# Moving TensorE's waits for the next projection ahead of the last chunk of the one before

## Chip, cores and metric

The kernel runs on one core of one Trainium2 chip. The metric is device time in microseconds (us) of one execution, from its first to its last instruction and what the measurement puts around them; the median of several runs counts.

## What is computed

Two transformer-like blocks, one layer each, on one sequence of 512 tokens with 1024 features, all in float32. Cut to the parts that matter here:

```python
# first block
h = modulate(rms_norm(x, g_ffn1), sh1, sc1)             # sh, sc, gt come from silu(c) @ w_ada + b_ada
x = x + 0.5 * gt1 * swiglu(h, w1_gu, w1_down)           # 1024 -> 2 x 2816 -> 1024
h = modulate(rms_norm(x, g_mix), sh2, sc2)
...                                                     # short convolution, windowed attention
merged = sigmoid(z_conv) * y_conv + sigmoid(z_attn) * y_attn
x = x + gt2 * (merged @ w_out)
h = modulate(rms_norm(x, g_ffn2), sh3, sc3)
x = x + 0.5 * gt3 * swiglu(h, w2_gu, w2_down)
# second block
x = x + token_mixer(rmsnorm(x, norm_mix), ...)          # HGRN and mLSTM heads
x = x + cross_attention(rmsnorm(x, norm_xattn), rmsnorm(mem, norm_mem), w_xq, w_xkv, w_xo)
h = rmsnorm(x, norm_mlp)
x = x + jnp.square(jax.nn.relu(h @ w_up)) @ w_down      # 1024 -> 4096 -> 1024
```

## The kernel before

Features lie on the 128 partitions, tokens along the row, so x is eight chunks of 128x512. Every projection is cut into units. A **unit** gives 128 output features for all 512 tokens in one PSUM bank: for each of its chunks of 128 input features (eight, or six in the down projections of the third part of a feed-forward) three matmuls accumulate, high weights by high input (L1439), high weights by low input (L1440), low weights by high input (L1441). That is how float32 accuracy comes from matmuls on a shorter format. There are 353 units, numbered v in the order in which they run: first feed-forward 0 to 67, then mix, convolution, its projection, attention's projection (`V_AP`, 120 to 135), output projection (`V_WO`, 136 to 143), second feed-forward (144 to 211), the mixer's (212 to 256), cross-attention's (257 to 280), its output projection (`V_XO`, 281 to 288) and the MLP (`V_MLP`, 289 to 352).

A unit's weights pass through four engines, each with its instructions in a fixed order, tied by semaphores:

- SyncE loads unit v's weights into one of four `raw` buffers (L342) when the buffer's last user is through.
- ScalarE (`split`, L428) rounds them into `whi[v % 2]` once unit v-2 has been multiplied (`unit_done`).
- VectorE (`split`, L820) writes the remainder into `wlo[v % 2]` and counts up `w_split`.
- TensorE (`unit`) waits for `w_split` and for `evac[v % 2]`, which says that bank v % 2 has been emptied of unit v-2, then multiplies, and counts up `unit_done` with the last matmul.

The two waits (L1428 to L1430) stand at the head of `unit`, ahead of the first chunk. Only the first unit that reads a new operand waits chunk by chunk as well (`first`), since its input is still being made.

What empties the bank depends on the stage. In a feed-forward, pairs of units (gate, up) are emptied by ScalarE (silu, L489) and VectorE (multiply, L917), and the product is split into `ghi` (L502) and `glo` (L923). A down projection's unit is added to x by VectorE (`residual`: L829 with a scale, L867 without). In the MLP an up unit goes through ScalarE (relu, L793), VectorE (square, L1405), ScalarE (`ghi`, L795) and VectorE (`glo`, L1407).

A feed-forward runs in three parts of 8, 8 and 6 chunks of 128 hidden features: 16, 16 or 12 gate and up units in a hardware loop, then eight down units. During the first feed-forward VectorE also multiplies the modulation weights `w_ada` (`ada`, one instruction L882 and seven L829 on 128x128, from the same four raw buffers), and TensorE adds each up with a matmul of one column (L1450) between two units. In a down projection VectorE's order for unit v is: split of v+1, residual of v, and for the first four units one `ada`. SyncE issues the loads in a fixed order too, so that the load of a down unit stands behind the load that waits for an `ada`.

The change touches `unit`, at the head of TensorE's program, and `mlp` at its end; both run through TensorE's loops (`Fori`), where the awaited counts are worked out in registers.

Of the kernel before, what the change touches and what calls it, by code (L numbers as in the profile page):

```python
# [24 lines left out]
DC = D // P  # L25
# [21 lines left out]
V_FFN_LEN = 2 * (FF // P) + len(FF_PARTS) * DC  # L47
# [3 lines left out]
V_AP = V_CP + 16  # L51
V_WO = V_AP + 16
V_FFN = (0, V_WO + DC)
V_GATE = V_FFN[1] + V_FFN_LEN
# [6 lines left out]
V_XO = V_XQ + DC  # L61
V_MLP = V_XO + DC
# [7 lines left out]
def raw_of(v):  # L70

    if v >= V_FFN_LEN:
        return v + N_ADA
    part = v // 24
    base, k, gu = ADA_HEAD_N + PART_LEN * part, v - 24 * part, 2 * FF_PARTS[part]
    return base + 2 * k if k < gu + ADA_TAIL else base + gu + ADA_TAIL + k


def raw_of_ada(a):
    if a < ADA_HEAD_N:  # L80
        return a
    part = sum(a >= start for start in ADA_PART[1:])
    return ADA_HEAD_N + PART_LEN * part + 2 * (a - ADA_PART[part]) + 1


def chunks_of(v):
    return FF_PARTS[2] if any(base + 60 <= v < base + V_FFN_LEN for base in V_FFN) else DC
# [27 lines left out]
def build(nc, x_in, mem_in, vec_in, con_in, rope_in, mask_in, w8_in, w6_in, out):  # L115
    with ExitStack() as ctx:
# [3 lines left out]
        def sem(name):  # L120
            return ctx.enter_context(nc.semaphore(name))
# [118 lines left out]
        w_split = sem("w_split")  # L240
        unit_done = sem("unit_done")
        evac = [sem(f"evac{i}") for i in range(2)]
# [92 lines left out]
        @block.sync  # L335
        def _(sp):
            sp.dma_start(vec[:], vec_in).then_inc(small_in, 16)

            def load(u, w, kc=DC):

                src = w8_in if kc == DC else w6_in
                sp.dma_start(raw[u % 4][:, 0:kc * P], src[w]).then_inc(landed[u % 4], 16)  # L342

            user = {raw_of(v): (w_split, v + 1) for v in range(V_END)}
            user |= {raw_of_ada(a): (ada_step, DC * (a + 1)) for a in range(N_ADA)}

            def load_at(u, w, kc=DC):
                if u >= 4:  # L350
                    sp.wait_ge(*user[u - 4])
                load(u, w, kc)

            for u in range(4):
                load_at(u, u)
            with sp.Fori(1, ADA_HEAD_N // 4) as i:
                for k in range(4):
                    sp.wait_ge(ada_step, DC * (k - 3) + 4 * DC * i)
                    load(k, 4 * i + k)
            for part, kc in enumerate(FF_PARTS):  # L360
                v0, a0 = 24 * part, ADA_PART[part]
                u0 = raw_of(v0)
                for u in range(u0, u0 + 8):
                    load_at(u, u)
                with sp.Fori(1, kc // 2) as i:
                    for k in range(4):
                        sp.wait_ge(w_split, v0 + k - 1 + 4 * i)
                        load(u0 + 2 * k, u0 + 2 * k + 8 * i)
                        sp.wait_ge(ada_step, DC * (a0 + k - 1) + 4 * DC * i)
                        load(u0 + 2 * k + 1, u0 + 2 * k + 1 + 8 * i)  # L370
                for c in range(DC):
                    u = raw_of(v0 + 2 * kc + c)
                    load_at(u, u if kc == DC else c, kc)
                    if c < ADA_TAIL:
                        load_at(u + 1, u + 1 if kc == DC else u0 + 4 * kc + c)

            def run(v0, v1, w0, kc=DC):

                for k in range(4):
                    load_at(raw_of(v0 + k), w0 + k, kc)  # L380
                if v1 - v0 >= 8:
                    with sp.Fori(1, (v1 - v0) // 4) as i:
                        for k in range(4):
                            sp.wait_ge(w_split, v0 + k - 3 + 4 * i)
                            load(raw_of(v0 + k), w0 + k + 4 * i, kc)
                for k in range((v1 - v0) // 4 * 4, v1 - v0):
                    load_at(raw_of(v0 + k), w0 + k, kc)

            down2 = V_FFN[1] + 60
            row0 = raw_of(V_MIX) - DC  # L390
            run(V_MIX, down2, row0)
            run(down2, V_GATE, DC, FF_PARTS[2])
            run(V_GATE, V_END, row0 + down2 - V_MIX)
            sp.wait_ge(stored, 16 * DC)
# [1025 lines left out]

        @block.tensor
        def _(pe):
            def unit(v, src, dv=0, n=S, first=None, rows=None):


                kc = chunks_of(v)
                hi, lo = src
                pe.wait_ge(w_split, v + 1 + 4 * dv)  # L1428
                if v >= 2 or not isinstance(dv, int):
                    pe.wait_ge(evac[v % 2], v // 2 + 2 * dv)  # L1430
                wh, wl = whi[v % 2], wlo[v % 2]
                outs = ((bank[v % 2], 0),) if rows is None else rows
                for dst, off in outs:
                    m = P if rows is None else 8
                    for c in range(kc):
                        if first is not None:
                            pe.wait_ge(first[0], first[1] + c + 1)
                        ws = slice(c * P + off, c * P + off + m)
                        nc.tensor.matmul(dst[0:m, 0:n], wh[:, ws], hi[:, c, :], start=c == 0, stop=False)  # L1439
                        nc.tensor.matmul(dst[0:m, 0:n], wh[:, ws], lo[:, c, :], start=False, stop=False)  # L1440
                        ins = nc.tensor.matmul(dst[0:m, 0:n], wl[:, ws], hi[:, c, :], start=False, stop=c == kc - 1)  # L1441
                ins.then_inc(unit_done, 1)
# [17 lines left out]
            def swiglu(f):  # L1460
                base, j0 = V_FFN[f], J_FFN[f]
                n = (N_FFN1, N_FFN2)[f]
                for part, kc in enumerate(FF_PARTS):
                    v0, j1, a0 = base + 24 * part, j0 + 8 * part, ADA_PART[part]

                    def body(i, first=None):
                        for k in range(4):
                            unit(v0 + k, H, i, first=first if k == 0 else None)
                            if f == 0 and (k >= 2 or not isinstance(i, int)):
                                ada(a0 + k - 2, 4 * i)  # L1470

                    if f == 0:
                        pe.wait_ge(mods_done, (2, 6, 7)[part])
                    body(0, (h_ready, H_AT[n]) if part == 0 else None)
                    with pe.Fori(1, kc // 2) as i:
                        body(i)
                    if f == 0:
                        for a in range(a0 + 2 * kc - 2, a0 + 2 * kc):
                            ada(a)
                    for c in range(DC):  # L1480
                        unit(v0 + 2 * kc + c, G, first=(op_ready, j1) if c == 0 else None)
                        if f == 0 and 2 <= c < 2 + ADA_TAIL:
                            ada(ADA_PART[part + 1] - ADA_TAIL + c - 2)
# [25 lines left out]
            for j in range(12):  # L1509
                unit(V_MIX + j, H, first=(h_ready, H_AT[N_MIX]) if j == 0 else None)  # L1510
                if 1 <= j <= 10:
                    rotate(j - 1)
                if j == 11:
                    v = V_MIX + 10
                    pe.wait_ge(evac[v % 2], v // 2 + 1)
                    turn_values(gate_in[0], bank[4], NB)
# [38 lines left out]
            v = V_MIX + 11  # L1555
# [176 lines left out]
            for c in range(DC + 4):  # L1732
                if c < DC:
                    unit(V_XQ + c, H, first=(h_ready, H_AT[N_XATTN]) if c == 0 else None)
                if c >= 2 and c % 2 == 0 and c < DC + 2:
                    hh = c // 2 - 1
                    v = V_XQ + c - 1
# [23 lines left out]


            def mlp(i, first):
                for c in range(DC):
                    unit(V_MLP + c, H, 4 * i, first=first if c == 0 else None)
                for c in range(DC):
                    unit(V_MLP + DC + c, G, 4 * i, first=(op_ready, J_MLP + DC * i) if c == 0 else None)

            mlp(0, (h_ready, H_AT[N_MLP]))
            with pe.Fori(1, MLP_PARTS) as i:  # L1770
                mlp(i, None)
# [126 lines left out]
```

## Time and profile before

| | |
|---|---|
| time, median of 3 runs | 2567.57 us |
| the runs | 2567.57, 2564.54, 2578.78 us |
| profiled execution, first to last instruction (span) | 2575.9 us |
| profiled execution's own time | 2578.78 us, the only one of the three above the span |
| TensorE busy | 2282.6 us, 89% |
| VectorE busy | 1320.8 us, 51% |
| ScalarE busy | 813.1 us, 32% |
| mean granted TensorE clock | 0.950 |
| HBM read | 226.45 MB |

PE is TensorE's matmuls, PEld its weight loads (LDWEIGHTS), DVE VectorE, ACT ScalarE, POOL GpSimd, SPq the queue that issues loads. Matmuls overlap: each is drawn as lasting 0.39 us or so, while the next starts 0.23 us after it, so the pace is read from starts and not from durations. A releaser behind "<-" is the instruction whose semaphore ended a wait.

### The profile page before, as it was taken

To read this page: it belongs to the slowest core of one execution; us is meant where nothing else is said; L and a number is where in the kernel's file an instruction comes from. 1 tells how busy PE (TensorE), PEld (TensorE's weight loads), DVE (VectorE), ACT (ScalarE), POOL (GpSimd) and SP (SyncE) were. 2 spreads that over 40 slices of the span, in tenths; PEclk is the share of its full clock that TensorE was granted. 3 is DMA by queue.
4 is the path that set the end of the run, shared out by engine and by line. 5 is a ranking of instruction groups with operands and counts; after the bars stand their busy time and mean duration, and the time that the engine had idled before them with its cause. 6 is when DMAs were issued, how large, how long until landed. Compare 5 with 4: busy or idle time off the path is not lost.

```text
span 2575.9 us, 27144 instructions
## 1 busy us (share of the span) xinstructions
PE 2282.6 (89%) x9880; PEld 1783.2 (69%) x9880; DVE 1320.8 (51%) x2228; ACT 813.1 (32%) x1174; POOL 83.3 (3%) x63
## 2 busy tenths in 40 slices
PE   1799999899999998999996788878868789899998
PEld 1588888676667776888883666655527666688886
DVE  7776768545554434333334455556554344534443
ACT  1322222323343323222234322224433343422332
POOL 1000000000000001000002000000000101000001
PEclk9899999999999999999998899988878999999999
DMA  6354544222122232333321111101103311233322
GB/s 230 122 173 162 177 164 165 91 79 66 58 72 80 78 90 74 98 98 98 95 88 56 58 41 40 39 28 41 46 3 98 115 50 63 74 94 104 93 95 73
DMA packets 63316, 229.92 MB, mean 89 GB/s; under 512 B 7024, under 2 KB 7152, under 8 KB 62960
## 3 DMA queue, kind: packets, MB, share of 16 engines
q1 hardware_dynamic: 61344, 220.90, 27.2%
q0 software_dynamic: 720, 5.57, 0.5%
q10 hardware_dynamic: 1152, 2.10, 0.2%
q8 instruction: 65, 1.06, 0.2%
q14 instruction: 35, 0.29, 0.0%
HBM read 226.45 MB, written 2.10 MB: 89 GB/s over the span
## 4 chain that ended last, share of the span: by engine, by line
PE 79%; DVE 12%; ACT 4%; issue 2%; POOL 1%; DMA 1%; DVEq 0%; SPq 0%; ACTq 0%; POOLq 0%
PE bank L1439 23%; PE bank L1440 23%; PE bank L1441 23%; DVE work L829 3%; PE bank L1643 2%; DVE normed L829 1%; PE bank L1526 1%; DVE hlo L829 1%; PE bank L1682 1%; PE bank L1551 1%; DVE work L1355 1%; PE bank L1666 1%; DVE wlo L820 1%; POOL square_sum L413 1%; PE bank L1709 1%
## 5 line engine op out<-in xcount | busy, mean ns | idle before, releaser
L1439 PE MATMUL bank<-hhi,whi 128*128 128x512 f32 (+1 forms) x1936 | 779.1, 402 | 80.5 <-DVE wlo L820 38.2
L1440 PE MATMUL bank<-hlo,whi 128*128 128x512 f32 (+1 forms) x1936 | 752.7, 389 | 0.0
L1441 PE MATMUL bank<-hhi,wlo 128*128 128x512 f32 (+1 forms) x1936 | 751.4, 388 | 0.0
L820 DVE TENSOR_TENSOR wlo<-raw,whi 128x1024 fp32r<-128x1024 f32 (+1 forms) x353 | 428.5, 1214 | 329.0 <-ACT whi L428 326.4
L1439 PEld LDWEIGHTS bank<-hhi,whi 128*128 128x128 f32 x1936 | 369.9, 191 | 197.9 <-issue 69.7
L428 ACT ACTIVATE whi<-raw 128x1024 fp32r<-128x1024 f32 (+1 forms) x353 | 368.0, 1042 | 434.9 <-PE bank L1441 392.2
L1441 PEld LDWEIGHTS bank<-hhi,wlo 128*128 128x128 f32 x1936 | 370.0, 191 | 76.2 <-issue 0.9
L1440 PEld LDWEIGHTS bank<-hlo,whi 128*128 128x128 f32 x1936 | 370.9, 192 | 73.2 <-issue 6.1
L1439 PE MATMUL bank<-ghi,whi 128*128 128x512 f32 x864 | 340.1, 394 | 6.2 <-DVE wlo L820 5.8
L1440 PE MATMUL bank<-glo,whi 128*128 128x512 f32 x864 | 336.6, 390 | 0.0
L1441 PE MATMUL bank<-ghi,wlo 128*128 128x512 f32 x864 | 336.5, 389 | 0.0
L829 DVE SCALAR_TENSOR_TENSOR work<-raw,cact,work 128x128 f32<-128x128 f32 x504 | 183.2, 363 | 17.9
L1439 PEld LDWEIGHTS bank<-ghi,whi 128*128 128x128 f32 x864 | 162.5, 188 | 42.1 <-DVE wlo L820 7.6
L1440 PEld LDWEIGHTS bank<-glo,whi 128*128 128x128 f32 x864 | 162.6, 188 | 33.7 <-issue 0.8
L1441 PEld LDWEIGHTS bank<-ghi,wlo 128*128 128x128 f32 x864 | 162.3, 188 | 34.0
L413 POOL TENSOR_TENSOR square_sum<-square_sum,square 128x512 f32<-128x512 f32 (+1 forms) x54 | 80.2, 1485 | 1932.7 <-ACT square L444 1929.5
L1643 PE MATMUL bank<-work 128*128 128x128 f32 (+1 forms) x512 | 78.5, 303 | 33.7 <-DVE work L1225 30.8
L829 DVE SCALAR_TENSOR_TENSOR xT<-bank,mods,xT 128x512 f32<-128x512 f32 x56 | 42.0, 750 | 123.8 <-PE bank L1441 123.8
L867 DVE TENSOR_TENSOR xT<-bank,xT 128x512 f32<-128x512 f32 x48 | 33.2, 691 | 137.9 <-PE bank L1441 137.9
L1643 PEld LDWEIGHTS bank<-work 128*128 128x128 f32 x512 | 68.2, 200 | 42.1 <-DVE work L1242 23.4
L502 ACT ACTIVATE ghi<-opnd 128x512 fp32r<-128x512 f32 (+1 forms) x44 | 27.8, 632 | 214.6 <-DVE opnd L917 214.6
L489 ACT ACTIVATE gate_in<-bank 128x512 f32<-128x512 f32 x44 | 26.4, 599 | 145.1 <-PE bank L1441 145.1
(186 smaller groups left out, 1595.2 us busy)
## 6 DMA issues: line engine op xcount, KB each, us to landing
raw<-w SPq DMA_DIRECT2D x409, 512.0 KB, 3.6
raw<-w SPq DMA_DIRECT2D x16, 384.0 KB, 3.1
xT<-x_t POOLq DMA_DIRECT2D x1, 2048.0 KB, 10.5
y_t<-xT ACTq DMA_DIRECT2D x8, 256.0 KB, 2.2
work<-mem_t POOLq DMA_DIRECT2D x1, 1024.0 KB, 5.0
con<-constants POOLq DMA_DIRECT2D x1, 960.0 KB, 13.4
work<-level_mask_in POOLq DMA_DIRECT2D x1, 896.0 KB, 18.2
work<-rope POOLq DMA_DIRECT2D x1, 512.0 KB, 15.4
```

Source lines behind the costliest of these rows:

```text
L413: nc.gpsimd.tensor_tensor(square_sum[:, 0:w], square_sum[:, 0:w], square[c % 2][:, 0:w], ALU.add).then_inc(sq_added, 1)
L428: nc.scalar.activation(whi[v % 2][:, 0:kc * P], raw[u % 4][:, 0:kc * P], ACT.Copy).then_inc(w_hi, 1)
L489: nc.scalar.activation(gate_in[k][:], bank[0][:], ACT.Silu).then_inc(evac[0], 1)
L502: nc.scalar.activation(ghi[:, g, :], opnd[k][:].unsqueeze(1), ACT.Copy).then_inc(op_hi, 1)
L820: nc.vector.tensor_tensor(wlo[v % 2][:, 0:kc * P], raw[u % 4][:, 0:kc * P], whi[v % 2][:, 0:kc * P].bitcast(F32), ALU.subtract).then_inc(w ...
L829: return nc.vector.scalar_tensor_tensor(out=out_ap, in0=in0, scalar=scalar, in1=in1, op0=op0, op1=op1)
L867: ins = nc.vector.tensor_tensor(xT[:, c, :], bank[v % 2][:], xT[:, c, :], ALU.add)
L1355: step(nc.vector.reciprocal(ml_h[dr], dmat[dr]))
L1439: nc.tensor.matmul(dst[0:m, 0:n], wh[:, ws], hi[:, c, :], start=c == 0, stop=False)
L1440: nc.tensor.matmul(dst[0:m, 0:n], wh[:, ws], lo[:, c, :], start=False, stop=False)
L1441: ins = nc.tensor.matmul(dst[0:m, 0:n], wl[:, ws], hi[:, c, :], start=False, stop=c == kc - 1)
L1643: ins = nc.tensor.matmul(b[:, k * w:(k + 1) * w], lhs, rhs, start=True, stop=True)
```

## The change

`early` names the units that wait on behalf of their successor: 0 to 66 (first feed-forward), 120 to 210 (attention's projection, output projection, second feed-forward), and 281 to 303 (cross-attention's output projection and the MLP's first round, whose numbers serve for all four rounds of its loop). For such a unit v, the two waits of unit v+1 stand ahead of the three matmuls of v's last chunk, and v+1 has none at its head. That holds for 226 boundaries between units. All others keep their waits where they were. In the MLP's loop the first unit of a round waits at the head of the round.

```diff
@@ tensor @@
-            def unit(v, src, dv=0, n=S, first=None, rows=None):
-
-
-                kc = chunks_of(v)
-                hi, lo = src
+            early = range(V_FFN_LEN - 1), range(V_AP, V_GATE - 1), range(V_XO, V_MLP + 2 * DC - 1)
+
+            def ready(v, dv):
+
                 pe.wait_ge(w_split, v + 1 + 4 * dv)
                 if v >= 2 or not isinstance(dv, int):
                     pe.wait_ge(evac[v % 2], v // 2 + 2 * dv)
+
+            def unit(v, src, dv=0, n=S, first=None, rows=None):
+
+
+                kc = chunks_of(v)
+                hi, lo = src
+                if not any(v - 1 in r for r in early):
+                    ready(v, dv)
                 wh, wl = whi[v % 2], wlo[v % 2]
@@
                     for c in range(kc):
                         if first is not None:
                             pe.wait_ge(first[0], first[1] + c + 1)
+                        if c == kc - 1 and any(v in r for r in early):
+                            ready(v + 1, dv)
                         ws = slice(c * P + off, c * P + off + m)
@@
             def mlp(i, first):
+                if first is None:
+                    ready(V_MLP, 4 * i)
                 for c in range(DC):
```

## Rows read from the trace of the kernel before

**Rows 1.** the page: span, busy time, costliest groups.

```profile
span 2575.9 us, 27144 instructions
PE 2282.6 (89%) x9880; PEld 1783.2 (69%) x9880; DVE 1320.8 (51%) x2228; ACT 813.1 (32%) x1174; POOL 83.3 (3%) x63
```

**Rows 2.** waits of TensorE's matmuls, whole span: who, total us, times, longest.

```profile
PE bank L1439 <- DVE wlo L820: 44.0, 19, 15.9
```

**Rows 3.** three windows: length, busy (x instructions) of PE, PEld, DVE, ACT, POOL; PEclk, DMA.

```profile
876.00:952.00 76.00, 76.00 (x337) 62.96 (x336) 26.21 (x28) 18.25 (x21) 0.00 (x0) 1.00 0.31 92
1021.50:1374.80 353.30, 353.30 (x1560) 292.55 (x1559) 127.71 (x134) 94.81 (x118) 9.46 (x6) 1.00 0.32 97
2220.00:2562.00 342.00, 342.00 (x1510) 283.17 (x1509) 141.42 (x157) 104.78 (x132) 10.32 (x6) 1.00 0.30 91
```

**Rows 4.** timeline around an MLP boundary (unit 308 starts at 2317.51): DVE, PEld, PE.

```profile
2315.33 1.23 DVE L820 TENSOR_TENSOR wlo<-raw,whi 128x1024 fp32r<-128x1024 f32 x1 [0.26 <-ACT whi L428]
...
2316.84 0.39 PE L1439 MATMUL bank<-hhi,whi 128*128 128x512 f32 x1
...
2317.29 0.19 PEld L1439 LDWEIGHTS bank<-hhi,whi 128*128 128x128 f32 x1
2317.51 0.39 PE L1439 MATMUL bank<-hhi,whi 128*128 128x512 f32 x1
```

**Rows 5.** timeline of a blocked boundary (unit 62, first feed-forward's third part): PE.

```profile
434.60 0.39 PE L1439 MATMUL bank<-ghi,whi 128*128 128x512 f32 x1
...
435.05 0.39 PE L1441 MATMUL bank<-ghi,wlo 128*128 128x512 f32 x1
435.99 0.50 PE L1439 MATMUL bank<-ghi,whi 128*128 128x512 f32 x1 [0.55 <-DVE wlo L820]
436.32 0.39 PE L1440 MATMUL bank<-glo,whi 128*128 128x512 f32 x1
```

**Rows 6.** timeline of the same part's down projection: DVE.

```profile
434.98 0.95 DVE L820 TENSOR_TENSOR wlo<-raw,whi 128x768 fp32r<-128x768 f32 x1
435.85 0.75 DVE L829 SCALAR_TENSOR_TENSOR xT<-bank,mods,xT 128x512 f32<-128x512 f32 x1
436.51 0.28 DVE L882 TENSOR_SCALAR work<-raw,cact 128x128 f32<-128x128 f32 x1
436.82 2.67 DVE L829 SCALAR_TENSOR_TENSOR work<-raw,cact,work 128x128 f32<-128x128 f32 x7
440.58 0.96 DVE L820 TENSOR_TENSOR wlo<-raw,whi 128x768 fp32r<-128x768 f32 x1 [1.09 <-ACT whi L428]
441.46 0.74 DVE L829 SCALAR_TENSOR_TENSOR xT<-bank,mods,xT 128x512 f32<-128x512 f32 x1
...
445.40 0.95 DVE L820 TENSOR_TENSOR wlo<-raw,whi 128x768 fp32r<-128x768 f32 x1
446.27 0.74 DVE L829 SCALAR_TENSOR_TENSOR xT<-bank,mods,xT 128x512 f32<-128x512 f32 x1
...
450.21 2.03 DVE L820 TENSOR_TENSOR wlo<-raw,whi 128x768 fp32r<-128x768 f32 x1
```

**Rows 7.** chain that ended last, the same part: start us, us, what.

```profile
435.46 4.23 DMA raw<-w
439.71 0.85 ACT whi L428
```

**Rows 8.** timelines, first part's down projection, boundary of units 18 and 19: DVE, PE.

```profile
191.33 1.22 DVE L820 TENSOR_TENSOR wlo<-raw,whi 128x1024 fp32r<-128x1024 f32 x1 [0.50 <-ACT whi L428]
...
191.72 0.39 PE L1439 MATMUL bank<-ghi,whi 128*128 128x512 f32 x1
```

**Rows 9.** waits of TensorE in short windows, at units 121 and 145.

```profile
PE bank L1439 <- DVE wlo L820: 1.9, 1, 1.9
...
PE bank L1439 <- DVE wlo L820: 0.5, 1, 0.5
```

**Rows 10.** window around unit 121's wait, columns as in Rows 3.

```profile
866.00:872.00 6.00, 4.09 (x18) 3.06 (x18) 5.94 (x9) 4.68 (x8) 0.00 (x0) 1.00 0.02 4
```

More of the change, by code:

```diff
@@ L1422, in _ @@
         def _(pe):
+            early = range(V_FFN_LEN - 1), range(V_AP, V_GATE - 1), range(V_XO, V_MLP + 2 * DC - 1)
+            def ready(v, dv):
+                pe.wait_ge(w_split, v + 1 + 4 * dv)
+                if v >= 2 or not isinstance(dv, int):
+                    pe.wait_ge(evac[v % 2], v // 2 + 2 * dv)
             def unit(v, src, dv=0, n=S, first=None, rows=None):
@@ L1427, in unit @@
                 hi, lo = src
-                pe.wait_ge(w_split, v + 1 + 4 * dv)
-                if v >= 2 or not isinstance(dv, int):
-                    pe.wait_ge(evac[v % 2], v // 2 + 2 * dv)
+                if not any(v - 1 in r for r in early):
+                    ready(v, dv)
                 wh, wl = whi[v % 2], wlo[v % 2]
```

## The prediction

> **What bounds the kernel now.** I read the page first. TensorE is busy for 2282.6 of a span of 2575.9 us, VectorE for half of it [rows 1], so whatever delays TensorE for good delays the end, and whatever fills a hole in it helps. The change moves waits of TensorE alone. The next question is therefore how long those waits last. The list of TensorE's waits has 44.0 us in 19 cases for "DVE wlo", the longest 15.9 us [rows 2]; these are the waits for split weights. That is all that a wait placed better could win, and moving a wait doesn't make VectorE's split finish sooner.
>
> Then I went through the boundaries that the change covers. In three windows (attention's projection, second feed-forward, MLP) TensorE is busy without a hole: 76.0 us for 337 matmuls, 353.3 us for 1560, 342.0 us for 1510 [rows 3]. Each comes to 0.226 us a matmul, boundaries included. A boundary seen close shows the same: the last chunk's first matmul starts at 2316.84, the next unit's first at 2317.51, 0.67 us or three matmuls later, and its weight load started at 2317.29, 0.22 us ahead of it, as inside a unit [rows 4]. In the 226 boundaries of the change I count 167 like this one. 42 more, all in the first feed-forward, have only the one-column matmul between the units and no wait. What is left are part changes, stage changes and the late splits below.
>
> **What the change does, and its terms.** No instruction is added to a unit: the same two waits are passed three matmuls earlier. Four cases follow, by how far the split's end R lies from the last chunk. Call L the time at which the last chunk would start by itself.
>
> *R well ahead of L.* Nothing changes. I worked L and R out for every boundary, from the split's line and the last chunk's first L1439 as in rows 4. In the second feed-forward the smallest usual margin L - R is 0.73 us (boundary 205 alone has 0.06), in its down projections it is 1.3 to 2.2 us. Cover: the queue of matmuls in front of the wait. Term: 0.
>
> *R just ahead of L.* In the MLP's up projections the split begins at 2315.33 and takes 1.23, so R is 2316.56, 0.95 us ahead of unit 308 but only 0.28 us ahead of the last chunk of unit 307 [rows 4]. 30 boundaries are like this, 5 with 0.28 us and 25 with about 0.37. The last chunk's weight load has to start at L - 0.22, that is 0.06 us (or 0.15) after R. In a blocked boundary the first matmul starts at 435.99 after R = 434.98 + 0.95 = 435.93, so the load goes out 0.06 us after R [rows 5, 6], just in time. An empty queue also costs a fill: the second matmul there starts 0.33 us after the first instead of 0.23, 0.11 us more [rows 5]. From below the price of such a boundary is 0; from above 0.11 us for the fill plus as much again for a register instruction between the two waits in the loop, so 0.2. I take 0, since by the measured 0.06 us the load is in time, and keep 30 x 0.2 = 6 us for the range.
>
> *R after L, VectorE not waiting for the unit next.* Today the unit is finished while the split runs and TensorE waits after it. With the change it waits in front of the last chunk, and these three matmuls run after R: three times 0.227, 0.68 us later; the fill is paid at either place. Unit 121 has such a wait (1.9 us as the gap between busy matmuls), units 145 and 290 another (0.5 each; the row of one stands) [rows 9]. What queues behind the wait is TensorE's own stream only, and the bank of the delayed unit has 2 us of slack or more at the following boundary. Term: 3 x 0.68 = 2.0 us. Unit 282's split ends 0.1 us after L: about 0.3 us with the fill.
>
> *R after L where VectorE waits for the very unit that now waits for VectorE.* This is the first feed-forward's down projections, and its third part is the worst. VectorE's order is split of v+1, residual of v, `ada`, split of v+2. Today residual follows the split at once (split to 435.93, residual at 435.85 as the trace overlaps them), because unit v was finished at 435.5. With the change unit v ends only after R: 0.06 until the last chunk, 0.34 + 0.23 to its third matmul, and 0.43 from there to the residual that waits for it, so R + 1.06. Step by step [rows 5 to 7]:
> - Boundary 62: R = 435.93 stays. Residual of 61 moves from 435.85 to 437.0, +1.15; unit 62 starts its steady run 0.68 later.
> - Boundary 63: ScalarE's rounding at 439.71 hangs on a load issued at 435.46, ahead of all this, so R stays near 441.55 (VectorE's `ada`, 0.28 + 2.67 after the residual, now ends at 440.7). Residual of 62 goes from 441.46 to 442.65, +1.2.
> - Boundary 64: VectorE runs without a gap, split at 445.40 + 1.2, R = 447.55. Residual of 63 goes from 446.27 to 448.6, +2.35.
> - Boundary 65: split at 450.21 + 2.35, R = 454.6. Unit 65's steady run is 2.35 + 0.68 = 3.0 us later. From here VectorE has no `ada` between and the splits are in time again.
>
> Each turn with both engines waiting thus costs more than the three matmuls. Term: 3.0 us. One split there lasts 2.03 us instead of 0.96 [rows 6]; if it no longer does, the term is 2.0.
>
> In the first part the split ends at 192.55, 0.83 after the last chunk of unit 18 (191.72) [rows 8]; boundaries 18 and 20 are late by 0.23 and 0.58. Some of it is taken up because the loads, not VectorE, set the next split. By the same walk unit 18 comes out 0.4 later, 19 by 0.9, 21 by 1.3. The second part is alike (late by 0.24, 1.04 and 0.28), 1.2 us. Term: 2.5 us.
>
> **Sum.** 0 + 2.0 + 0.3 + 3.0 + 2.5 = 7.8 us slower. After each of these stretches TensorE runs densely, so nothing gives it back. The profiled execution took 2578.8 us, 11.2 above the median; the stretches used are the same work in any run, so I add 7.8 to the median 2567.6: **2575.4 us**. A measurement of this kernel tells about 0.5%, 12.8 us, from no change (the three runs lie 14 us apart), so the forecast is a small loss that counts as no change.
>
> **A rule against the rows.** What a wait in front of a unit could cost is shown by the blocked boundary, 0.11 us of fill [rows 5], and the unblocked one doesn't pay it [rows 4]. The Trainium skill, TensorE: Matmul & The Clock Gate, "LDWEIGHTS (loading the stationary operand)", gives a weight load about its columns over 1.2 GHz, some 107 ns, and "Step-by-step: what each phase is for" says that TensorE pulls such loads ahead of matmuls in flight. If a wait at a unit's head kept that from happening, taking it away would gain about 226 x 0.107 = 24 us, an estimate by that page; the trace has the load 0.22 us ahead already.
>
> **Rivals.**
> - *The tight MLP boundaries are late* (slower). If the sequencer needs longer than 0.15 us to get going after R, every one of the 30 pays, and since the next split hangs on the end of the delayed unit, the margin never recovers. It decides from (12.8 - 7.8) / 30 = 0.17 us each; at 0.2 us the sum is 13.8, time 2581.4. For it: 0.06 us of room at five of them, the loop's register work. Against: the measured 0.06 us. Chance 0.14.
> - *The clock falls in the third part* (slower). By the walk above unit 64's last chunk waits from 451.9 to 454.65, 2.8 us. Around unit 121 a wait of 1.9 us passed at a granted 1.00 [rows 9, 10], 2.4 GHz; a longer one in this part has no row. At 1.2 GHz a matmul takes 0.23 us more; some 20 of them make 4.6 us, time 2580. Chance 0.04.
> - *The head wait holds the pipeline, and moving it frees it* (faster). 0.11 us at each of 226 boundaries, 25 us, so 2575.4 - 25 = 2550. Against it stands the even pace of rows 3. Chance 0.03.
> - *The loss is taken up* (no change). The loads and not the splits pace the first feed-forward, and only the isolated boundaries pay: 2.3 us, 2570. For it: boundary 63, where the load decides. Chance 0.12.
> - My forecast: 0.67.
>
> **Range and chances.** From the rival that is taken up, with some room for the scatter of runs, to the tight boundaries at 0.2 us and the fallen clock together, 18 us: 2566 to 2586. Faster by over 0.5%: 0.03. Slower by over 0.5%: the first rival, the second added to my sum's upper end, and a little for scatter: 0.16. Within: 0.81.
>
> **What the profile after would show.** The even pace of 0.226 in the three windows, down to the MLP; if the tight boundaries pay, MLP matmuls of 0.33 us spacing appear in the last chunks. Waits for "DVE wlo" sit three matmuls ahead of a unit's end, and the gaps at the starts of units 121, 145 and 290 are gone. In the third part VectorE idles about 1 us before each of three residuals, where it idled at none, and unit 66 starts 3 us later relative to unit 60. Wrong would be any gain in the second feed-forward, or a loss there.

## The result: 0.3% slower

| | before | changed |
|---|---|---|
| median of 22 runs each | 2573.34 us | 2580.95 us |
| lowest to highest | 2560.58 to 2580.97 | 2574.22 to 2589.47 |
| ratio, 95% interval | | 1.0032 (1.0020 to 1.0045) |
| profiled execution's span | 2575.9 us | 2572.1 us |

The loss is small but real: the interval of the ratio lies above 1, and on 2573.34 us it is 8.2 us (5.1 to 11.6); the two medians themselves lie 7.6 us apart. It is below the 0.5% from which the prediction would have called it a change. One run of the kernel before, taken beside the first experiments, lasted 8700.42 us at a granted clock of 0.463 and is left out.

The profiled execution of the changed kernel is still shorter than that of the kernel before, so whoever compares the two spans draws the wrong conclusion. Two windows show why; the first is of the kernel before, the second of the changed kernel. Each begins and ends within 0.6 us of the starts of units 222 and 223 (1504.17 and 1525.43 before, 1512.42 and 1529.49 after), in the HGRN stage, which the change doesn't touch. The columns are those of rows 3.

```profile
1504.00:1526.00 22.00, 17.80 (x61) 11.85 (x60) 9.40 (x25) 0.69 (x1) 0.00 (x0) 0.77 0.09 25
```

```profile
1512.00:1530.00 18.00, 13.80 (x63) 10.01 (x63) 9.65 (x27) 0.69 (x1) 0.00 (x0) 1.00 0.08 30
```

From start to start the same work takes 21.3 us at a mean granted clock of 0.77 and 17.1 us at 1.00. In this stage TensorE works in short bursts between waits, and whether the clock is at 2.4 or 1.2 GHz for the closing matmuls differs from one execution to the next, in kernels that are alike in this stage. At three such places (before units 223, 228 and 233) the time from the last matmul of one unit to the first of the next is 15.6 to 16.0 us in the profiled execution of before and 11.7 us in this one, 12.2 us together, more than the change costs. So the cost is read stretch by stretch, and the total from the 22 runs.

The page of the changed kernel, the lines that answer to [rows 1]:

```profile
span 2572.1 us, 27164 instructions
PE 2273.4 (88%) x9880; PEld 1776.4 (69%) x9880; DVE 1320.3 (51%) x2228; ACT 813.2 (32%) x1174; POOL 83.1 (3%) x63
```

As many matmuls as before, and 20 instructions more, in all queues. TensorE's waits, whole span, answer to [rows 2]; the matmuls L1439 to L1441 are L1448 to L1450 now:

```profile
PE bank L1448 <- DVE wlo L820: 46.5, 19, 15.9
```

The sum grew from 44.0 to 46.5 us, in as many cases. Windows with the same content as in [rows 3]:

```profile
882.00:952.00 70.00, 70.00 (x310) 57.95 (x310) 24.99 (x27) 16.70 (x19) 0.00 (x0) 1.00 0.31 98
1030.00:1378.00 348.00, 348.00 (x1536) 288.04 (x1535) 124.60 (x132) 92.07 (x114) 7.66 (x5) 1.00 0.32 96
2224.00:2554.00 330.00, 330.00 (x1457) 273.14 (x1457) 137.79 (x153) 100.72 (x127) 9.04 (x5) 1.00 0.30 91
```

348 us for 1536 matmuls and 330 us for 1457 are 0.2266 and 0.2265 us each: the same even pace. Nothing was won at the boundaries, and nothing lost at those of the MLP. The cost must lie outside these three windows.

**Stretch by stretch.** For each kernel I took the start of the first matmul of unit a and of unit b from the timeline, and their difference. In the kernel before, unit 60 starts at 427.0 and unit 66 at 456.7, 29.68 us; in the changed one 429.2 and 461.15, 31.94 us. All kernels of this study:

```
us from the start of unit a to the start of unit b
                       16-24  40-48  60-66  120-122 144-148 148-212 289-293 293-352
before                 45.79  46.05  29.68  13.23   27.36   364.14  27.37   320.96
changed                46.96  47.36  31.94  13.95   29.77   364.30  29.77   321.08
e10 changed, again     47.12  47.19  33.60  13.93   28.15   364.29  29.74   321.01
e1 third part only     45.86  46.11  31.92  14.87   27.37   364.15  27.37   320.96
e2 stage starts only   45.77  45.96  29.53  15.57   29.66   364.14  29.68   320.96
e3 late ones spared    45.80  46.11  29.51  13.23   27.49   364.30  27.47   321.01
e4 MLP, two chunks     45.92  45.96  28.54  13.27   27.37   364.15  31.48   336.98
e5 ada first           45.70  45.71  28.79  13.23   27.37   364.15  27.37   320.96
e6 ada first, changed  45.70  45.70  28.46  13.91   29.73   364.31  28.16   320.98
e7 no stage starts     47.21  47.23  33.59  15.27   27.46   364.31  27.46   321.01
e8 one matmul held     45.87  46.11  29.61  15.06   27.61   364.14  27.61   320.96
e9 ada first, ffn1     45.69  45.70  28.55  13.27   27.37   364.14  27.39   320.96
```

16-24, 40-48 and 60-66 are the down projections of the first feed-forward's three parts; 144 and 289 are the first units of the second feed-forward and of the MLP. Where a kernel's code is as before, the numbers repeat to 0.2 us, with two exceptions. 60-66 lies between 28.54 and 29.68 (e2, e3, e4, e8 and before), and 120-122 is 13.2 where nothing is changed or, with the low clock there, 1.3 to 1.6 more (e1; e2, e7 and e8 have it on top of their wait).

One stretch that the change covers is missing from the table: 136-143, the output projection. It takes 40.92 us in the kernel before, 38.83 in the changed one and 39.84 in e10, and what differs is mostly the clock at unit 136. Two windows of kernels with the old code at this place, the kernel before and e9:

```profile
955.00:963.00 8.00, 7.19 (x20) 5.69 (x21) 6.01 (x9) 4.53 (x8) 0.00 (x0) 0.59 0.12 16
```

```profile
955.00:963.00 8.00, 6.79 (x30) 5.64 (x31) 6.79 (x10) 5.91 (x10) 0.00 (x0) 1.00 0.10 10
```

With the clock up through unit 136 the old code needs 38.20 us (e9), the changed one 38.83 and, in e6, 38.84. So boundary 137 joins the late ones when the clock is up, and costs 0.63 us. In the trace before its split was 2.4 us ahead of the last chunk, because unit 136 ran at the low clock.

**The third part.** VectorE's timeline in the changed kernel, against [rows 6]:

```profile
437.18 0.95 DVE L820 TENSOR_TENSOR wlo<-raw,whi 128x768 fp32r<-128x768 f32 x1
439.20 0.75 DVE L829 SCALAR_TENSOR_TENSOR xT<-bank,mods,xT 128x512 f32<-128x512 f32 x1 [1.07 <-PE bank L1450]
439.87 0.28 DVE L882 TENSOR_SCALAR work<-raw,cact 128x128 f32<-128x128 f32 x1
440.18 2.67 DVE L829 SCALAR_TENSOR_TENSOR work<-raw,cact,work 128x128 f32<-128x128 f32 x7
442.79 0.96 DVE L820 TENSOR_TENSOR wlo<-raw,whi 128x768 fp32r<-128x768 f32 x1
444.81 0.75 DVE L829 SCALAR_TENSOR_TENSOR xT<-bank,mods,xT 128x512 f32<-128x512 f32 x1 [1.06 <-PE bank L1450]
...
448.38 0.95 DVE L820 TENSOR_TENSOR wlo<-raw,whi 128x768 fp32r<-128x768 f32 x1
450.40 0.75 DVE L829 SCALAR_TENSOR_TENSOR xT<-bank,mods,xT 128x512 f32<-128x512 f32 x1 [1.06 <-PE bank L1450]
```

Where residual followed the split without a gap, it now waits 1.06 us each time for the matmuls that waited for that split. And the start of a stage, here the end of unit 144 and the head of unit 145, TensorE:

```profile
1023.38 0.50 PE L1448 MATMUL bank<-hhi,whi 128*128 128x512 f32 x1 [0.47 <-DVE hlo L829]
1023.72 0.40 PE L1449 MATMUL bank<-hlo,whi 128*128 128x512 f32 x1
1023.96 0.39 PE L1450 MATMUL bank<-hhi,wlo 128*128 128x512 f32 x1
1025.74 0.66 PE L1448 MATMUL bank<-hhi,whi 128*128 128x512 f32 x1 [1.39 <-issue]
1026.20 0.63 PE L1449 MATMUL bank<-hlo,whi 128*128 128x512 f32 x1
1026.62 0.63 PE L1450 MATMUL bank<-hhi,wlo 128*128 128x512 f32 x1
```

The unit's last chunk begins at 1025.74, 1.78 us after the matmul in front of it, and its matmuls follow each other by 0.42 to 0.46 us. The profile names no releaser, but VectorE's split of unit 145 ends at 1025.64, 0.10 us ahead:

```profile
1024.41 1.23 DVE L820 TENSOR_TENSOR wlo<-raw,whi 128x1024 fp32r<-128x1024 f32 x1 [0.20 <-ACT whi L428]
```

The window behind has the clock:

```profile
1026.00:1029.00 3.00, 3.00 (x8) 2.32 (x8) 0.14 (x1) 1.54 (x2) 0.00 (x0) 0.50 0.50 175
```

0.50 is 1.2 GHz. In the kernel before, unit 145 starts at 1021.12, and the clock is at 1.00 from 1021.5 on [rows 3]. That was not in my sum.

### The profile page after: what moved, and what is told of

Its sections match the earlier page's. It is cut to its first block, busy times and chain, and to the rows that moved or that the text cites. A ratio compares the mean times of both kernels' runs of the same rounds, so it can differ in the third digit from the quotient of the medians.

```text
span 2572.1 us, 27164 instructions
## 1 busy us (share of the span) xinstructions
PE 2273.4 (88%) x9880; PEld 1776.4 (69%) x9880; DVE 1320.3 (51%) x2228; ACT 813.2 (32%) x1174; POOL 83.1 (3%) x63
## 3 DMA queue, kind: packets, MB, share of 16 engines
q8 instruction: 65, 1.06, 0.2%
## 4 chain that ended last, share of the span: by engine, by line
PE 79%; DVE 12%; ACT 4%; issue 3%; POOL 1%; DMA 1%; DVEq 0%; SPq 0%; POOLq 0%; ACTq 0%
PE bank L1448 24%; PE bank L1450 23%; PE bank L1449 23%; DVE work L829 3%; PE bank L1652 2%; DVE normed L829 1%; DVE hlo L829 1%; PE bank L1535 1%; PE bank L1691 1%; PE bank L1560 1%; DVE work L1355 1%; DVE wlo L820 1%; POOL square_sum L413 1%; PE bank L1718 1%; DVE work L1242 1%
## 5 line engine op out<-in xcount | busy, mean ns | idle before, releaser
L1448 PE MATMUL bank<-hhi,whi 128*128 128x512 f32 (+1 forms) x1936 | 779.3, 403 | 85.1 <-DVE wlo L820 39.9
L1450 PE MATMUL bank<-hhi,wlo 128*128 128x512 f32 (+1 forms) x1936 | 752.0, 388 | 0.0
L1448 PEld LDWEIGHTS bank<-hhi,whi 128*128 128x128 f32 x1936 | 369.3, 191 | 202.9 <-issue 58.5
L1450 PEld LDWEIGHTS bank<-hhi,wlo 128*128 128x128 f32 x1936 | 369.7, 191 | 76.6 <-issue 0.6
L1448 PE MATMUL bank<-ghi,whi 128*128 128x512 f32 x864 | 341.3, 395 | 7.1 <-DVE wlo L820 6.6
L1450 PE MATMUL bank<-ghi,wlo 128*128 128x512 f32 x864 | 336.7, 390 | 0.0
L1448 PEld LDWEIGHTS bank<-ghi,whi 128*128 128x128 f32 x864 | 162.5, 188 | 46.4 <-DVE wlo L820 11.8
L1450 PEld LDWEIGHTS bank<-ghi,wlo 128*128 128x128 f32 x864 | 162.4, 188 | 34.2
L1652 PE MATMUL bank<-work 128*128 128x128 f32 (+1 forms) x512 | 73.2, 290 | 33.7 <-DVE work L1225 30.8
## 6 DMA issues: line engine op xcount, KB each, us to landing
con<-constants POOLq DMA_DIRECT2D x1, 960.0 KB, 13.2
```

What stands on the lines that cost most here:

```text
L1652: ins = nc.tensor.matmul(b[:, k * w:(k + 1) * w], lhs, rhs, start=True, stop=True)
```

## The experiments

The theory to test: a boundary costs nothing unless the split ends behind the new place of the wait; then it costs the matmuls that are held back, more where VectorE in turn waits for that unit, and a clock that falls comes on top in some places. Each kernel differs from before or from the changed one only as its diff shows.

**e1, the third part alone.**

```diff
-            early = range(V_FFN_LEN - 1), range(V_AP, V_GATE - 1), range(V_XO, V_MLP + 2 * DC - 1)
+            early = (range(61, 65),)
```

> Only boundaries 62 to 65 wait early (down projection of the first feed-forward's third part). My theory (VectorE waits for the very unit that waits for VectorE, so each turn costs more than three matmuls): against before, in the trace, unit 62 starts 0.7 to 0.8 us later, 63 0.8 to 1.0, 64 1.5 to 2.0, 65 and 66 1.4 (with one long split shorter) to 3.0 us later, and nothing before unit 62 moves. Rival (the wait only changes places, the loads set the pace): unit 66 starts 0.7 us later at most.

Measured: 31.92 us for units 60 to 66, as 31.94 in the changed kernel; against before, 2.2 us more, against the other kernels with the old code there 2.3 to 3.4. Units 62 to 66 start 0.8, 0.9, 1.7, 2.3 and 2.2 us later. The rival, 0.7 us at most, is out. The size is near the lower of my two values, the one with the long split shorter: the split that lasted 2.03 us [rows 6] takes 0.95 here. The four late boundaries cost 0.8, 0.1, 0.8 and 0.6 us; the one that costs next to nothing is 63, where the load decides.

**e2, the stage starts alone.**

```diff
-            early = range(V_FFN_LEN - 1), range(V_AP, V_GATE - 1), range(V_XO, V_MLP + 2 * DC - 1)
+            early = ((V_AP, V_FFN[1], V_MLP),)
```

> Only the units 120, 144 and 289 (289 in every round of the MLP's loop) make the early waits. My prediction's theory: three matmuls, 0.7 us, at each of boundaries 121, 145 and 290, and nothing in the later MLP rounds. Rival, formed from the changed kernel's trace, which showed 2.4 us at 145 and at 290: with the wait inside the thinly filled first unit of a stage, the clock stays at or falls back to 1.2 GHz for another 3 to 7 us, so the following unit runs partly at 0.43 us a matmul: about 2.4 us at 145 and at 290, 0.7 at 121, where TensorE had been dense before.

Measured: 144-148 takes 2.30 us more than before, 289-293 2.31. My prediction's 0.7 fails, the rival from the changed kernel's trace stands. Unit 121 starts 0.82 us later. The stretch 120-122 is 2.3 us longer, of which 0.7 is the hold and 1.6 the low clock behind it. e1 has the same 1.6 with the old code at this place, in the window behind a wait of 1.91 us:

```profile
882.00:886.00 4.00, 4.00 (x13) 3.12 (x12) 0.00 (x0) 0.00 (x0) 0.00 (x0) 0.57 0.74 254
```

**e8, one matmul held back instead of three.** The wait stands between the last chunk's second and third matmul, in the same three units.

```diff
-            early = range(V_FFN_LEN - 1), range(V_AP, V_GATE - 1), range(V_XO, V_MLP + 2 * DC - 1)
+            early = ((V_AP, V_FFN[1], V_MLP),)
@@
-                        if c == kc - 1 and any(v in r for r in early):
-                            ready(v + 1, dv)
                         ws = slice(c * P + off, c * P + off + m)
@@
+                        if c == kc - 1 and any(v in r for r in early):
+                            ready(v + 1, dv)
                         ins = nc.tensor.matmul(dst[0:m, 0:n], wl[:, ws], hi[:, c, :], start=False, stop=c == kc - 1)
```

> Units 120, 144 and 289 wait for their successor ahead of their last matmul alone, not of their last three (e2_stage_starts). Theory (a late boundary pays for the matmuls that are held back): about 0.23 us at boundary 121, 0.2 to 0.3 at 145 and at 290. Rival (what costs at 145 and 290 is the clock, which falls once the last matmuls of that thin unit run late): 0.23 plus about 1.6 us at 145 and at 290, as with three held.

Measured: 0.25 us at either stage start, 27.61 against 27.36 and 27.37. TensorE at the boundary, and the windows around it:

```profile
1026.18 0.50 PE L1446 MATMUL bank<-hhi,whi 128*128 128x512 f32 x1
1026.52 0.40 PE L1447 MATMUL bank<-hlo,whi 128*128 128x512 f32 x1
1027.61 0.50 PE L1450 MATMUL bank<-hhi,wlo 128*128 128x512 f32 x1 [0.69 <-DVE wlo L820]
1027.94 0.40 PE L1446 MATMUL bank<-hhi,whi 128*128 128x512 f32 x1
```

```profile
1022.00:1028.00 6.00, 4.08 (x14) 2.10 (x14) 5.16 (x7) 4.13 (x5) 0.00 (x0) 1.00 0.00 0
1028.00:1034.00 6.00, 6.00 (x28) 4.95 (x27) 1.55 (x2) 1.55 (x2) 0.00 (x0) 1.00 0.59 169
```

So a late boundary costs one matmul's 0.23 us for each one held back, and at both stage starts the clock stayed up. At boundary 121 it didn't: unit 121 starts 0.33 us later, and 120-122 has the low clock on top, as in e1. With three held it fell at six of eight stage starts, two each in four kernels (changed, e2, e6, e10), and the boundary cost 2.3 to 2.4 us; in the other two (e10 at 145, e6 at 290) it stayed up and the cost was 0.79. The clock's records agree: behind each of the six holds they have 3.4 us at half speed, behind the other two none. An estimate from this: 3.4 us of matmuls at half pace lose 1.7 us, and 2.3 to 2.4 less 0.79 is 1.5 to 1.6. By the same records the clock had risen 4.3 to 4.9 us after the start of the stage's first unit in the six, and 5.5 and 6.2 us after it in the two. What exactly the chip reacts to isn't settled by these runs.

**e7, the changed kernel without the two stage starts.**

```diff
-            early = range(V_FFN_LEN - 1), range(V_AP, V_GATE - 1), range(V_XO, V_MLP + 2 * DC - 1)
+            early = (range(V_FFN_LEN - 1), range(V_AP, V_FFN[1]), range(V_FFN[1] + 1, V_GATE - 1), range(V_XO, V_MLP),
+                     range(V_MLP + 1, V_MLP + 2 * DC - 1))
```

> The changed kernel, but units 144 and 289 (the thin first units of the second feed-forward and the MLP) wait at the old place. Theory: the 2.3 to 2.4 us that boundaries 145 and 290 cost there are the 0.7 us of three matmuls and a later rise of the clock, both brought by the wait inside that unit, so against before neither boundary shifts by more than 0.1 us now, and the granted clock is 1.00 from 2 us before unit 146 on. Rival (the clock's rise there is a matter of phase, as elsewhere in this kernel): a shift of 1 us or more remains at one of them or at both.

Measured: 27.46 at both, 0.1 us over before. The theory holds: the early wait inside the first unit is what brings the 2.3 us there. But 60-66 took 33.59 us, 1.65 more than in the changed kernel's first trace with the same code. e10 shows the same and where it comes from.

**e10, the changed kernel once more.** No edit.

> The changed kernel once more. Theory: the shifts that are no matter of the clock repeat to 0.2 us: about 1.2 in the first part's down projection, 1.3 in the second's, 2.2 in the third's (near 4 if the clock falls in its longest wait, as in one run so far), 0.7 at 121 (more if the clock is low there), 0.3 at 282. Boundaries 145 and 290 cost 2.3 to 2.4 each if the clock falls again, 0.7 or 0.8 if not.

Measured: 1.33, 1.14 and 3.92 us in the three parts, 0.70 at 121, 0.29 at 282 (from the shift of unit 282 against 281), 0.79 at 145 and 2.37 at 290. TensorE in the longest wait of the third part, and the windows before and behind it:

```profile
455.12 0.39 PE L1450 MATMUL bank<-ghi,wlo 128*128 128x512 f32 x1
457.38 0.50 PE L1448 MATMUL bank<-ghi,whi 128*128 128x512 f32 x1 [1.87 <-DVE wlo L820]
457.72 0.45 PE L1449 MATMUL bank<-glo,whi 128*128 128x512 f32 x1
457.97 0.63 PE L1450 MATMUL bank<-ghi,wlo 128*128 128x512 f32 x1
458.40 0.42 PE L1459 MATMUL bank<-con,work 128*128 128x1 f32 x2
458.68 0.77 PE L1448 MATMUL bank<-ghi,whi 128*128 128x512 f32 x1
459.25 0.63 PE L1449 MATMUL bank<-glo,whi 128*128 128x512 f32 x1
```

```profile
446.00:458.00 12.00, 9.16 (x42) 6.97 (x41) 9.45 (x20) 2.73 (x4) 3.47 (x3) 1.00 0.40 134
458.00:462.00 4.00, 4.00 (x13) 3.25 (x12) 1.71 (x2) 1.36 (x2) 1.54 (x1) 0.58 0.93 338
```

After 2.26 us without a new matmul (1.87 us by the profile's ends) the clock falls, from 458 on 0.58 on the mean. In two of four traces with this wait it fell (e7, e10), in two it didn't (changed, e1), for 1.66 us (33.60 less 31.94).

**e3, the change without its 16 late units.**

```diff
-            early = range(V_FFN_LEN - 1), range(V_AP, V_GATE - 1), range(V_XO, V_MLP + 2 * DC - 1)
+            late = {17, 18, 19, 20, 41, 42, 43, 44, 61, 62, 63, 64, V_AP, V_FFN[1], V_XO, V_MLP}
+            whole = range(V_FFN_LEN - 1), range(V_AP, V_GATE - 1), range(V_XO, V_MLP + 2 * DC - 1)
+            early = tuple([v for v in r if v not in late] for r in whole)
```

> The change, but 16 units whose successor's split came late (17 to 20, 41 to 44, 61 to 64, 120, 144, 281, 289) keep the old place of the wait. My theory (only late splits cost): in the trace every unit up to the first change of the clock starts where it did before, within 0.1 us plus the start's own scatter, and the ratio to before is 1.000 within its interval. Rival 1 (the 30 tight MLP boundaries cost): MLP 3 to 6 us longer. Rival 2 (a wait at a unit's head held back its weight load): 0.1 us gained at each of some 200 boundaries, 20 us faster.

Measured: ratio 1.0012 (0.9994 to 1.0030), and in the trace no unit starts more than 0.25 us away from where it starts in the kernel before, over the whole span; this execution happened to have the same clock. Span 2576.0 against 2575.9. Both rivals are out: some 200 early waits neither gain nor cost, all tight MLP boundaries among them. (Counted again, these are 31, not 30: 5 with 0.28 us and 26 with 0.37.) This window of e3 repeats the third of [rows 3] to the matmul:

```profile
2220.00:2562.00 342.00, 342.00 (x1510) 283.14 (x1509) 141.52 (x157) 104.81 (x132) 10.32 (x6) 1.00 0.30 91
```

**e4, the MLP's waits ahead of the last two chunks.**

```diff
-            early = range(V_FFN_LEN - 1), range(V_AP, V_GATE - 1), range(V_XO, V_MLP + 2 * DC - 1)
+            early = (range(V_MLP, V_MLP + 2 * DC - 1),)
@@
-                        if c == kc - 1 and any(v in r for r in early):
+                        if c == kc - 2 and any(v in r for r in early):
```

> Only the MLP waits early, and ahead of its last two chunks instead of the last. The split's end then lies 0.3 to 0.4 us behind that place at 30 boundaries. My theory (a boundary pays what the split is late, plus 0.06 and 0.11 us of fill, and the next split hangs on the end of the delayed unit, so that the lateness stays): about 0.5 us each, 15 us, plus about 1.4 us or more at boundary 290; MLP up units take 5.9 us instead of 5.44, down units 5.44. Rival (the split catches up after the first late one, or the queue hides it): under 2 us in all.

Measured: ratio 1.0071 (1.0049 to 1.0094), 18 us; in the trace the MLP from unit 293 on takes 336.98 instead of 320.96 us, each up unit whose successor's split is late costs 0.50 to 0.67 us, down units 0.00. Boundary 290 costs 3.0, with the clock down behind it. One of the late places, VectorE's split and TensorE:

```profile
2320.03 1.23 DVE L820 TENSOR_TENSOR wlo<-raw,whi 128x1024 fp32r<-128x1024 f32 x1 [0.26 <-ACT whi L428]
```

```profile
2320.65 0.39 PE L1450 MATMUL bank<-hhi,wlo 128*128 128x512 f32 x1
2321.39 0.49 PE L1448 MATMUL bank<-hhi,whi 128*128 128x512 f32 x1 [0.35 <-DVE wlo L820]
2321.72 0.39 PE L1449 MATMUL bank<-hlo,whi 128*128 128x512 f32 x1
```

The split ends at 2321.26, the matmul starts at 2321.39, 0.13 us later, against 0.06 in straight-line code [rows 5, 6]. The same trace compares the two: in the MLP's first round, which stands outside the loop, units 291 to 296 resume 0.05 or 0.06 us after the split, in the loop it is 0.05 and 0.13 in turn. So 0.07 us more go with the loop at every second late boundary; that the register work is the reason is likely and not shown. 0.74 instead of 0.23 before it and 0.33 instead of 0.23 behind it make 0.61. So the price that I had set for the tight boundaries' worst case was of the right kind, a late resumption and a fill; it isn't paid in the changed kernel since 0.28 us and more of margin are left.

**e5 and e6, VectorE's order turned**, in the kernel before and in the changed one.

```diff
                         split(v + c + 1)
-                        residual(v + c, c, mod(2 if f == 0 else 8, c))
                         if f == 0 and c < ADA_TAIL:
                             ada(ADA_PART[part + 1] - ADA_TAIL + c)
+                        residual(v + c, c, mod(2 if f == 0 else 8, c))
```

> The kernel before, with VectorE's order in the first feed-forward's down projections turned: ada ahead of the residual, which waits for the unit. My theory (there the split comes late because ada, and the load queued behind it, start only after the residual): ada moves up into VectorE's idle time before the residual (4.3 us in the first part), the loads follow it, and the waits at boundaries 19, 43 and 62 to 65, 5.5 us together beyond the pace, shrink to 1 to 2 us: unit 66 starts 3 to 4.5 us earlier, ratio 0.998 to 0.999. Rival (memory or ScalarE sets the pace, or the residual, now later, holds the bank and the norm): 0 to 2 us either way.

> The changed kernel with the same turned order. If the cost in the first feed-forward is that VectorE waits for the unit that waits for VectorE, it should mostly go with ada out of that loop: unit 66 starts within 1 us of where it starts in e5_ada_first, against 4.5 us of difference between before and after with the old order. Rival (each late boundary costs three matmuls, wherever ada stands): still 3 us or more behind e5_ada_first.

Measured: e5 has the ratio 0.9993 (0.9975 to 1.0011). The three parts take 0.1, 0.3 and 0.9 us less, the last within what this stretch varies by itself. My 3 to 4.5 us were wrong, the rival's 0 to 2 is right. VectorE's timeline of e5 shows why:

```profile
440.00 0.96 DVE L820 TENSOR_TENSOR wlo<-raw,whi 128x768 fp32r<-128x768 f32 x1 [1.71 <-ACT whi L428]
440.87 1.31 DVE L882 TENSOR_SCALAR work<-raw,cact 128x128 f32<-128x128 f32 x1
442.22 2.68 DVE L829 SCALAR_TENSOR_TENSOR work<-raw,cact,work 128x128 f32<-128x128 f32 x7
444.81 0.75 DVE L829 SCALAR_TENSOR_TENSOR xT<-bank,mods,xT 128x512 f32<-128x512 f32 x1
445.47 0.95 DVE L820 TENSOR_TENSOR wlo<-raw,whi 128x768 fp32r<-128x768 f32 x1
```

From 440.00 on VectorE has no idle time: this turn of split, `ada` and residual is 5.47 us of its own work, about 1 us of it the first `ada` instruction's 1.31 instead of 0.28, while six chunks on TensorE take 4.1. In the third part it is then the bound by its own work.

e6 is the test of the mechanism. Early waits cost nothing in its first feed-forward, 28.46 us against 28.79 for the third part and the same 45.70 in the others, where the old order paid 1.17, 1.31 and 2.26. There are two reasons. In the first and second part the splits now end 1.6 to 2.4 us ahead of the last chunk, so that no boundary is late. In the third part TensorE still waits for the split at units 62 to 64, its last chunks starting 0.06 us after the split's end. But VectorE does `ada` while the held matmuls run, and its residual follows without a wait:

```profile
437.22 0.74 DVE L829 SCALAR_TENSOR_TENSOR xT<-bank,mods,xT 128x512 f32<-128x512 f32 x1
443.25 0.75 DVE L829 SCALAR_TENSOR_TENSOR xT<-bank,mods,xT 128x512 f32<-128x512 f32 x1
```

So the next split is not put off. The stage starts cost in e6 as they did (2.37 and 0.79).

**e9, the parts that the traces favour:** the turned order of e5, and early waits in the first feed-forward alone.

```diff
-            early = range(V_FFN_LEN - 1), range(V_AP, V_GATE - 1), range(V_XO, V_MLP + 2 * DC - 1)
+            early = (range(V_FFN_LEN - 1),)
```

> ada ahead of the residual, and the early waits in the first feed-forward alone: the best of the parts by the traces so far. Expected: unit 66 starts 1.3 to 1.7 us earlier after unit 1 than in the kernel before, nothing else moves; the ratio to before lies between 0.998 and 1.001, within what a measurement tells. Rival: the early waits cost again, unit 66 later than before.

Measured: unit 66 starts 1.56 us earlier after unit 1, the ratio is 1.0001 (0.9990 to 1.0012). Its interval ends below that of the changed kernel (1.0020 to 1.0045), so it is better than that one; no version of this study is measurably better than the one before.

## Why the prediction was right, and where not

I forecast 7.8 us more, 0.30%; measured were 8.2 us (5.1 to 11.6), 0.32%. The absolute time of 2580.95 lies in my range too, but 2573.34 for the kernel before, with 19 further runs, is 5.8 above the median that I started from. Term by term, from the two traces of the changed kernel against before:

| term | forecast | changed | e10 |
|---|---|---|---|
| steady boundaries, units 148 to 212 and 293 to 352 | 0 | 0.28 | 0.20 |
| boundary 121 | 0.68 | 0.72 | 0.70 |
| boundary 282 | 0.3 | 0.29 | 0.29 |
| boundaries 145 and 290 | 1.36 | 4.81 | 3.16 |
| first and second part | 2.5 | 2.48 | 2.47 |
| third part | 3.0 | 2.26 | 3.92 |
| sum | 7.8 | 10.8 | 10.7 |

- **No gain at 167 even boundaries:** right, and it was the main thing to see. The load of the next unit's weights had gone out 0.22 us ahead already [rows 4], so there was nothing that a wait moved forward could set free. e3 shows it over the whole kernel. The estimate of 24 us took 107 ns for a weight load of 128 columns from the Trainium skill, TensorE: Matmul & The Clock Gate, "LDWEIGHTS (loading the stationary operand)". The trace draws one as 0.19 us [rows 4], which decides, and would have made it 43 us. That a wait at a unit's head holds the load back was my supposition, and the trace before and e3 both speak against it.
- **The tight MLP boundaries:** right at 0. e4 shows that the margin decides: with 0.68 us less of it the same boundaries cost 0.5 to 0.67 us each.
- **Late boundaries of which nothing else hangs:** right, three matmuls, 0.68 forecast and 0.70 to 0.79 measured with the clock up. e8 confirms the price per matmul held.
- **Boundary 137:** not in my sum. The trace before has its split well ahead of the last chunk, which holds only while unit 136 runs at the low clock. Where the clock is up it is late and costs 0.63 us; this is not in the table either.
- **Boundaries 145 and 290:** the step that failed. I took "three matmuls" from a case with the clock up and applied it to a unit that starts a stage, whose chunks wait one by one for the norm. A fall of the clock I expected in the third part alone. With three matmuls moved behind the wait it fell at six of eight such places and cost 1.6 us beyond.
- **Third part:** the mechanism is right to the detail (VectorE idles 1.06 us before each residual, as worked out; boundary 63 costs nearly nothing; e6, where VectorE no longer stands idle ahead of the residual and `ada`, pays nothing). Its size without a fall of the clock is 2.2 to 2.3 us. The step that was off is the long split: I left it at 2.03 us, and it was 0.95 in the new timing, as my lower value allowed. The rival with the clock was given 0.04, and it came in two of four traces, at 1.66 us instead of 4.6; it deserved more. I had leaned on one trace in which a wait of 1.9 us at unit 121 passed at full clock [rows 10]. In e1 the clock fell behind the same wait in the same code.
- **The sum** hit the median's change partly by luck: one term was 1.8 to 3.5 us too small, another up to 0.9 off either way. The traces' 10.8 and 10.7 lie above the measured 8.2 and within its interval. With the output projection, which was 2.1 and 1.1 us shorter through the clock, and with 0.1 us gained at each of three changes of stage, all stretches that the change covers come to 8.5 and 9.4 us. The rest of the kernel keeps its own scatter through the clock. From unit 212 to unit 257 the changed kernel is 11.1 us and e10 10.9 us shorter than the kernel before; e1 and e9, with the old code from unit 120 on, are 4.5 us shorter, and e3, e4 and e5 are as before. I can't tell from these runs whether the change shifts the mean there.

## What to carry to other kernels

A wait moved forward can only win where the trace shows a hole behind it; where starts follow each other at the inner pace across the boundary, the queue hides the wait and there is nothing to win. It costs the time of the instructions that are put behind it whenever the awaited thing comes late, so look for the late cases first, and above all for those where the one that is awaited waits in turn for what is now held back. Where the scatter of runs is larger than the effect, compare stretches between two marked instructions in the traces, and look at the clock in each before believing a total.

## What the hardware showed that I had not expected

- The clock makes much of the scatter of this kernel. Over the 22 runs of the changed kernel a run's time and its mean granted clock have a correlation of -0.71, over 46 runs of the kernel before taken beside the experiments -0.69. The clock's mean is 0.954 in both, so the loss of 8.2 us isn't a lower clock over the whole kernel. In its profiled execution the kernel before spent 262 us at 1.2 GHz, the changed one 231 us, summed over the clock's records, mostly in stages of bursts in which the code doesn't differ.
- A hold of 1.8 to 2.3 us, from one matmul's start to the next, let the clock fall in some traces and not in others: in two of four in the third part, in six of eight at the stage starts. At unit 121 the profile gives the wait as 1.9 to 2.6 us; the clock fell at its end in e1, e2, e7 and e8 and stayed up in the other eight traces. The length of the hold alone doesn't decide it: in e1 1.91 us were enough, in the changed kernel 2.59 were not.
- Some of VectorE's instructions stretch when they start while GpSimd adds. In e5 the `ada` instruction that takes 0.28 us elsewhere takes 1.31 and starts inside this one of GpSimd:

```profile
440.56 1.53 POOL L413 TENSOR_TENSOR square_sum<-square_sum,square 128x512 f32<-128x512 f32 x1 [418.64 <-ACT square L444]
```

  The split of 2.03 us in [rows 6] starts at 450.21, inside such an add (450.07 to 451.42); in the changed kernel the split at 448.38 runs already when the add begins at 448.94, and takes 0.95. In the trace before, among instructions of VectorE with at least five alike, 17 start during such an add, and 13 of them are stretched, by 0.4 to 1.1 us; the other four read a PSUM bank. Of 34 that run already when an add begins, none is stretched by over 0.3 us, and none that meets no add. No run here takes GpSimd's work away to prove the cause.
